# A PEER layer on one core: an early fetched tile in the routing stage, and a dense stage that steps all fetched tiles together with U in three fp32r passes

## What is computed

```
def blk(tb):                                   # 128 tokens
    q = (tb @ wq).reshape(128, 8, 2, 128)
    sc = einsum('thpd,pnd->thpn', q, subkeys)
    sv, si = top_k(sc, 16)
    cand = sv[:,:,0,:,None] + sv[:,:,1,None,:]
    cv, ci = top_k(cand.reshape(128, 8, 256), 16)
    e = i1 * 128 + i2                          # 128 experts a token, of 16384
    g = softmax(cv)
    h = einsum('thkd,td->thk', u[e], tb)
    a = gelu(h) * g
    return einsum('thk,thkd->td', a, v[e])
```

## Time and profile before

| | us |
|---|---|
| median of 3 runs | 3752.91 (3752.08 to 3759.64) |
| profiled execution | 3756.75 |
| its span, first to last instruction | 3755.0 |
| start of the dense stage in it | 1906 |
| start of the last PE instruction | 3745 |
| TensorE clock, mean granted share | 0.958 |

### The profile page before, as it was taken

The page is one execution under the profiler, slowest core; times in us unless marked ns, Lnnn a source line. Parts: engine busy times, 40 slices in busy tenths (PEclk is TensorE's granted clock), DMA queues, the critical chain, the costliest instruction groups (busy, mean ns, idle before and its releaser), DMA issues.

```text
span 3755.0 us, 45250 instructions
## 1 busy us (share of the span) xinstructions
PE 3435.2 (91%) x14374; PEld 2026.9 (54%) x14374; DVE 2662.5 (71%) x4988; ACT 890.0 (24%) x1844; POOL 1447.1 (39%) x1116
## 2 busy tenths in 40 slices
PE   8998989986889998999549999999999999999998
PEld 7444879884466667677414444444444444444443
DVE  0453887756368755655768888887888888889786
ACT  1452211215122338797100000100001000100001
POOL 0000187740232778874023343333343334333331
PEclk8899999988899999999779999999999999999999
DMA  7898499975887668888679999999999999999994
GB/s 262 342 421 298 136 401 378 378 275 168 322 311 252 170 179 182 193 147 190 205 285 398 406 398 390 398 390 391 409 385 400 406 397 418 401 399 365 387 379 185
DMA packets 470727, 1201.16 MB, mean 320 GB/s; under 512 B 196953, under 2 KB 261897, under 8 KB 391817
## 3 DMA queue, kind: packets, MB, share of 16 engines
q0 software_dynamic: 149776, 679.68, 47.7%
q1 hardware_dynamic: 187200, 498.50, 35.7%
q10 hardware_dynamic: 133568, 20.84, 3.5%
HBM read 1127.33 MB, written 72.61 MB: 320 GB/s over the span
## 4 chain that ended last, share of the span: by engine, by line
PE 32%; DVE 8%; issue 4%; DMA 4%; DVEq 1%; POOL 1%; POOLq 0%
PE d_ps L2482 17%; PE d_ps L2471 15%; DVE d_acc L2367 4%; DMA d_ring<-peer_uv,d_idx 3%; DVE d_ring L2353 3%; DMA out_y<-k_yacc 1%; DVE d_qacc L2384 1%; DVE k_yacc L2367 1%; POOL d_ring L2315 0%; DVE d_aw L2362 0%; DVE d_a L2375 0%; DVE d_qacc L2413 0%; DVEq L2362 0%; DVEq L2353 0%; DVEq L2366 0%
## 5 line engine op out<-in xcount | busy, mean ns | idle before, releaser
L2315 POOL DMA_INDIRECT d_ring<-peer_uv,d_idx x512 | 654.3, 1278 | 1067.1 <-DVEq L2369 964.1
L2471 PE MATMUL d_ps<-k_xd,k_ring 128*128 128x512 f32 x2048 | 907.0, 596 | 74.6 <-SPq L2283 60.4
L2471 PEld LDWEIGHTS d_ps<-k_xd,k_ring 128*128 128x128 f32 x2048 | 391.5, 191 | 569.4 <-issue 508.3
L2353 DVE SCALAR_TENSOR_TENSOR d_ring<-d_ring,k_xn 128x1024 f32<-128x1024 f32 x512 | 605.6, 1219 | 70.2 <-DMA d_ring<-peer_uv,d_idx 39.5
L2482 PE MATMUL d_ps<-d_v,d_a 128*128 128x512 f32 x1024 | 456.9, 600 | 32.5 <-DVE d_a L2375 24.6
L2482 PE MATMUL d_ps<-k_ring,d_a 128*128 128x512 f32 x1024 | 451.7, 594 | 16.1 <-DVE d_a L2375 16.1
L1630 POOL DMA_INDIRECT G<-c_cellg,c_cell x256 | 420.2, 1641 | 116.8 <-issue 90.1
L2367 DVE SCALAR_TENSOR_TENSOR d_acc<-d_ring,d_aw,d_acc 128x1024 f32<-128x1024 f32 x256 | 328.8, 1284 | 49.9 <-DVE d_acc L2367 32.3
L2367 DVE SCALAR_TENSOR_TENSOR k_yacc<-d_ring,d_aw,k_yacc 128x1024 f32<-128x1024 f32 x256 | 328.7, 1284 | 47.8 <-DVE k_yacc L2367 31.7
L2482 PEld LDWEIGHTS d_ps<-d_v,d_a 128*128 128x128 f32 x1024 | 196.3, 193 | 284.7 <-issue 283.4
L2438 ACT ACTIVATE d_ge<-d_h (+1 forms) x256 | 52.1, 203 | 1238.6 <-DVE d_ring L2353 1238.5
(11 more groups left out here) (382 smaller groups left out, 4442.3 us busy)
## 6 DMA issues: line engine op xcount, KB each, us to landing
c_chunk<-wq SPq DMA_DIRECT2D x128, 512.0 KB
k_ring<-u_blocks SPq DMA_DIRECT2D x128, 512.0 KB, 12.7
s_kc<-sb_kT SPq DMA_DIRECT2D x32, 1024.0 KB, 9.1
s_vc<-sb_v SPq DMA_DIRECT2D x32, 1024.0 KB, 7.3
c_chunk<-w_m SPq DMA_DIRECT2D x64, 512.0 KB
k_ring<-v_blocks SPq DMA_DIRECT2D x64, 512.0 KB, 13.4
d_gb<-G SPq DMA_DIRECT2D x32, 1024.0 KB
d_v<-v_blocks SPq DMA_DIRECT2D x64, 512.0 KB
```

Of the source, the lines that this page charges most:

```text
L2315: pool.indirect_dma_start(out=ring[:, b], out_offset=None, in_=a["peer_uv"], in_offset=bass.IndirectOffsetOnAxis(ap=idx8[par][:, b:b + 1], ...
L2353: last = nc.vector.scalar_tensor_tensor(ring[:, b, 0:D], ring[:, b, 0:D], 1.0, xn[T % 2][:], ALU.mult, ALU.mult, accum_out=h[:, bass.ds(co ...
L2471: last = nc.tensor.matmul(ps[:, HB + x % 2, :], ub[j][:, k], xd[:, k].rearrange("p t q -> p (t q)"), start=(k == 0), stop=(k == KC - 1))
```

## The change

In `decide`:

- The order of fates: tile 1 is now a fetched one; sent are tiles 2 and 4, hot 3 and 5, fetched 1, 6, 7, 8. `TILE` maps places in the intermediate buffers back to tiles.
- Tile 1's normed inputs stay in `c_xn0`. DVE's new `dots` multiplies its 128 fetched U rows (512 KB a slot) by them into `k_h0`: 16 in stage 4, 26, 31 and 33 in stages 5, 6 and 7, 22 in stage 8. The rows pass through three slots of the ring (`EB`). A row's gather waits until the dot three before it is done.
- POOL's queue: 19 of those gathers ahead of the first scatter, then one after each scatter with s % 5 in (0, 2, 4) of the first sent tile, and after s % 4 == 1 of the second: 19, 77 and 32. The two sent tiles' heads no longer take turns.
- One-hot chunks are moved between places, eight of them into the selection after the loop; six chunk buffers for weights become five; eight of the 56 V gathers for the sampled tile move forward into stage 2.

In `dense`:

- All fetched tiles step together: per PE block one 1 MB gather for each of tiles 6 to 8 and one 512 KB gather of V rows for tile 1, whose hidden values are already there. The ring of eight becomes two buffers per tile (`both`) and a single one for tile 1 (`values0`).
- `hidden` in three passes: ACT rounds a U block to fp32r (`u_high`), DVE subtracts (`low`, `u_low`), PE does 16 matmuls of `u_high` with both parts of the inputs and 8 of `u_low` with the high part.
- `values`: four of the eight outputs of a group stay in PSUM over the whole stage (`HELD`), so `take` runs four times a group.

```
+    BETWEEN, DOTS, DOTS_BESIDE = 29, {4: 16, 5: 20, 6: 19, 7: 21, 8: 10}, {5: 1, 6: 2, 7: 2, 8: 2}
-    NB = 6
+    NB = 5
     RB = 6
+    EB, EARLY_AT = 3, 3
...
+                def early_rows(n):
+
+                    for k in range(asked[0], min(asked[0] + n, P)):
+                        if k >= EB:
+                            pool.wait_ge(dotted, k - EB + 1)
+                        pool.indirect_dma_start(out=ring[:, EARLY_AT + k % EB], out_offset=None, in_=rows,
+                                                in_offset=bass.IndirectOffsetOnAxis(ap=row0[:, k:k + 1], axis=0)).then_inc(filled[EARLY_AT + k % EB], 16)
+                        asked[0] = k + 1
+
+                pool.wait_ge(rows_ready, 1)
+                pool.wait_ge(summed, REST)
+                early_rows(DOTS[4] + EB)
...
-                for h in range(4):
-                    scatter_head(0, h)
-                for h in range(4):
-                    scatter_head(1, h)
-                    scatter_head(0, h + 4)
-                for h in range(4):
-                    scatter_head(1, h + 4)
+                        if s % rows_after[0] in rows_after[1]:
+                            early_rows(1)
+
+                for h in range(8):
+                    scatter_head(0, h, (5, (0, 2, 4)))
+                for h in range(8):
+                    scatter_head(1, h, (4, (1,)))
+                early_rows(P)
...
+                def dots(n):
+
+                    for k in range(dots_done[0], dots_done[0] + n):
+                        s = EARLY_AT + k % EB
+                        dve.wait_ge(filled[s], 16 * (len(range(s, REST, RB)) + k // EB + 1))
+                        nc.vector.scalar_tensor_tensor(ring[:, s], ring[:, s], 1.0, xn0[:], ALU.mult, ALU.mult, accum_out=h0[:, k:k + 1]).then_inc(dotted, 1)
+                    dots_done[0] += n
...
+                        due = DOTS.get(i, 0)
+                        dots(due * passed[0] // BETWEEN - due * (passed[0] - 1) // BETWEEN)
...
                         one_hots(k)
+                        dots(DOTS_BESIDE.get(i, 0))
```

and in `dense`, on DVE, ACT and PE:

```
+                def low(b, j):
+
+                    dve.wait_ge(u_high_done, b + 1)
+                    if not (number(b) and b == 0):
+                        dve.wait_ge(h_done, b)
+                    nc.vector.tensor_tensor(u_low[:], ub[j], u_high[:].bitcast(F32), ALU.subtract).then_inc(u_low_done, 1)
...
+                            products(k, x)
                             gate(b - 1, y // GB, y % GB, k if x else k - 1)
...
+                            low(b, j)
+                        n = 2 * k + u - 1
+                        if j in (1, 2) and not (number(n) and n < 0):
+                            for c in (2 * j - 2, 2 * j - 1):
                                 take(n, c)
...
+                        add_rows(k, x)
...
                     for k in range(KC):
-                        last = nc.tensor.matmul(ps[:, HB + x % 2, :], ub[j][:, k], xd[:, k].rearrange("p t q -> p (t q)"), start=(k == 0), stop=(k == KC - 1))
+                        for n, x_part in enumerate((x_high, x_low)):
+                            last = nc.tensor.matmul(ps[:, HB + x % 2, :], u_high[:, k], x_part[:, k], start=(k == 0 and n == 0), stop=False)
+                    last.then_inc(high_used, 1)
+                    pe.wait_ge(u_low_done, b + 1)
+                    for k in range(KC):
+                        last = nc.tensor.matmul(ps[:, HB + x % 2, :], u_low[:, k], x_high[:, k], start=False, stop=(k == KC - 1))
```

## The result

The changed kernel takes 3887.22 us (median of 4 runs, 3884.22 to 3891.12); its ratio to the kernel before is 1.0356 (95% interval 1.0338 to 1.0374), so it is 3.6% slower. 3828 us was forecast, with a range of 3725 to 3965. The profiled execution has a span of 3889.4 us. The dense stage starts at 2199 us (forecast 2132, before 1906) and lasts 1690 us (forecast 1698, before 1849). So the dense stage gained 159 us as worked out, the routing stage lost 293 instead of 226, and the error of 59 us is 67 in the routing stage less 8 in the dense one.

The account below looks back on a forecast made before the run. PE was taken to bound the dense stage before, POOL's queue the changed routing stage. Dense start 2132 (226 later) plus 1698 dense (151 less) gives a 3830 span, 3828 us against the median, 2.0% slower; range 3725 to 3965.

Parts of the forecast that it names:

- PE's block of 12.31 us: Dense stage: PE's time per block falls from 13.73 to 12.31 us, as hidden takes 5.44 us instead of 6.87.
- The loop through the landings: Dense stage: issue, landing and gathers' data against shallow buffers add 0 to 1.4 us a block over 12.31; 0.5 taken.
- the low end: Dense block: period of 12.1 us with none of SP's 1.31 MB in the way, so no wait over 12.31.
- Head: Start of the dense stage until the first values: 75 us, before 73.
- fourth case: Rival, dense stage: loop bound by landings, 13.7 us a block instead of 12.8, 112 us more, 3940 us; chance 0.15.
- The takes: Dense block: DVE's takes wait for PE's block end, using most of 1.1 us of room; costed at nothing.
- POOL's sum: Routing stage: scatters, gathers and waits in POOL's queue take 743 us from 1254.4, ending at 1997; taken as the limit.
- 3 x 5 us at changes of stage: Routing stage: at three changes DVE's work between takes about 20 us against 15 for POOL's three rows and scatters.
- Alone this would add some 15 us: Routing stage: the 128 dots cost DVE 151 us; if POOL did not hold the stage, they would add some 15.
- up to some 10 us: Routing stage: five chunk buffers, moved V gathers and PE's clock costed at nothing; each up to this if POOL didn't hold it.
- POOL keeps up: Rival, routing stage: POOL's instructions cost less between gathers; delay about 50 us, 3652 us, or 3617 with only 15; chance 0.20.
- third case: Rival, routing stage: rough handover, POOL loses 25 us more at each of four changes of stage, 3928 us; chance 0.14.

Follow-up runs that it names:

- two passes: Changed kernel with the eight u_high times x_low matmuls per block left out, x_low still made: 3888.96 us, ratio 1.0357 to the kernel before.
- scatters alone: Changed kernel without the 128 early U-row gathers and without 127 of their 128 products on DVE: 3628.03 us, ratio 0.9672 to the kernel before.
- the two kernels without rows: Changed kernel without the 128 early U-row gathers, once with the products on DVE kept (3685.62 us), once with 127 of 128 left out too (3628.03 us).
- the kernel without the rows: Changed kernel without the 128 early U-row gathers, scatters kept, products still run on what lies in the slots: 3685.62 us, ratio 0.9787 to the kernel before.
- even rates: Changed kernel with three early rows after every seven scatters in both sent tiles and products of stages 6, 7, 8 at 17, 17, 16: 3862.68 us, ratio 1.0309.

## Why the prediction came out as it did

Slower was the likeliest case, with POOL's queue in the routing stage as the reason, and the runs show that reason: left alone with either half of its queue, POOL does not hold the stage. The size of the loss was too small: 75 us were forecast and 135 came. The forecast for the dense stage is close in part by luck: the period was 0.13 us longer than forecast, 16 us over the stage, and the head and the end were each some 12 us shorter. Step by step:

*Dense stage.* PE's block of 12.31 us: 12.32 where PE alone bounds. The loop through the landings, with ends of 12.1 and 13.7 us a block: 12.10 with the loads taken away, which is the low end's condition, and 12.93 with them, where 12.8 was taken. Head: 63 us to the first values (2199.2 to 2262.6) for 75. Stage: 1690 us for 1698. The subtraction is 1.22 us for 1.15. The prediction had this loop as a term on top of PE's block, and as its fourth case at full size. The runs show that the loop sets the period and PE's block does not (12.95 with two passes); the half microsecond that was taken over 12.31 was a choice between two ends that no row decided. The takes were costed at nothing; nothing in the waits speaks against it (1.7 us of idle time before them in 1300).

The Trainium skill ("DMA: Bandwidth & Descriptors", section on SWDGE vs HWDGE vs iDMA) says that GpSimd's queue and the hardware's share each DMA engine in turns. The prediction put the sum by it near 3940, but that is its 13.7 us a block, worked out with half of the loads in the way; all 1.31 MB at 417 GB/s would be 3.1 us, a block of 15.2. The loads lengthened the block by 0.83 us (12.10 to 12.93), about half of the 1.6 of the first and a quarter of the second, so an effect is there, but much smaller than loads fully in the way.

*Routing stage.* POOL's sum is the term that failed, by 73 us. It was 743 us from 1254.4, end at 1997; it was 796 us from 1274.5, end at 2070.4 (the last scatter starts at 2068.8). By parts:

| part of POOL's sum | forecast us | measured us |
|---|---|---|
| start of the scatters | 1254.4 | 1274.5 |
| scatters with the gap behind each, waits between heads | 573 | 446.4 + 73.7 + 43.5 = 563.6 |
| 109 gathers | 145 | 133.1 + 29.9 = 163.0 |
| waits for products | 25 | 69.2 |
| sum | 743 | 795.8 |

The scatters' cost hit by two errors that cancel: a scatter's mean was 1.74 us, not 1.62, so scatters and gaps were 520 us for 494, and the waits between heads were 43.5 us for the 79 in the sum, since gathers stand in them. A gather was 1.22 us (133.1/109), not 1.08. The first wait for a product was 23.9 us for 25. The step that was mis-sized most is the wait for products after it: 45 us in ten waits where none was in POOL's sum. It was reasoned about only on DVE's side, 3 x 5 us at changes of stage. 36 of the 45 us stand in one place, at and just behind the change from stage 6 to 7 (22.1, 4.9, 5.2 and 4.2 us). The start was 20 us late with tile 2's weights: 1259.6 without rows and products, 1266.8 with the products, 1274.5 with both. Stage 4 already holds 16 products, and the sum had taken the weights' time from before.

*Behind POOL.* The last residual came 11 us after POOL's last scatter (forecast 26), the dense stage 120 us after it (forecast 109; before 103). The 120 are not POOL's: they are 117.5 us in the kernel with scatters alone, so 14 of the 35 us that go to the new order and the buffers lie here.

*Products on DVE.* "Alone this would add some 15 us" was too low: 49 us by the two kernels without rows. The 35 us for all that was costed at nothing in this stage (order of tiles, chunk buffers) were within the "up to some 10 us" each only if there are three or four of them. Whether they show in the total while POOL holds the stage was not tried, but both belong in the case in which POOL keeps up: that rival's 3617 us would have been about 3686, which is what the kernel without the rows takes; it could hardly come out otherwise, as both corrections are from that kernel and the one with scatters alone.

**The signs.** POOL's last scatter near 2000: 2069. DVE idle for U rows, 60 to 100 us in each of stages 7 and 8: 87 and 98. PE under 75%: 61 and 65%. Of the third case's sign, POOL idle over 20 us at each change of stage, there were two, at the first (23.9, which the sum had) and from stage 6 to 7 (22.1); from 5 to 6 it was 7.2, from 7 to 8 none. That case would have added 100 us; 45 came. Of the fourth's, DVE waits for gathers in most blocks, the waits are there (142 in 128 blocks), but the DMA share is 0.98, not under 0.95. It reads 0.98 to 1.00 also where engines are not what limits, so it was no good sign. Here the prediction's fourth case was right in its mechanism and small in its size.

**The rival that POOL keeps up** rested on 1.4 us an instruction; 365 instructions took 796 us, 2.2 each, and 1.87 without any wait for a product or a landing. The Trainium skill (same page, "Latency and other measured facts") gives about 1 us of emission for a DMA from GpSimd. The scatter's median was 1.58 us, its mean 1.74: for scatters the trace does not agree. For the gathers of rows it does, with a median of 1.01 us.

None of these kernels that computes the whole layer beats the kernel before; the best, with even rates, is 3.1% slower.

## What to carry to other kernels

Slack of a queue engine is eaten at the price of its whole instruction, with the gap behind it and its mean rather than its median, and by the waits of an in-order partner: 109 gathers in a queue with 160 us of slack cost 163 us themselves and 69 us of waits, and DVE, which consumes them, stood for 285 us. Price such a move by leaving out each half of the queue in turn: here the rows cost some 30 to 45 us without the scatters and 210 us among them. In a loop whose buffers are one or two deep, work out the way from the last use through the issue and landing to the next use; it gave 12.1 us for the 12.10 measured without direct loads, and with them only two ends, 12.3 and 13.7, for 12.93. The share of busy transfer engines suggested a bound that removing bytes did not confirm.

## What the runs showed of the hardware

- A stretch with 0.98 of the DMA engines busy and 385 to 388 GB/s was not at their limit for this loop: with 0.26 MB of direct loads a block less it was 358 to 365 GB/s at a share of 0.92 to 0.94, and the block did not get shorter (13.09 us for 12.93).
- Three gathers of 8 KB rows and one of 4 KB rows a block, with nothing beside them, moved 305 GB/s at a share of 0.84, and the former took 8.4 us to land (median; 9.3 with 1.31 MB of direct loads a block beside them).
- TensorE's granted clock was 1.00 in the dense stage with PE busy for 97%, and 0.94 to 0.96 with the pass taken out and PE busy for 87 to 88% (2300 to 3300). PE's block of 10.5 us would be 81% of the period of 12.95, so part of what the shorter block frees went with the lower clock. In the routing stage it fell from 1.00 in stage 7 to 0.79, with PE busy for 61%.
- A scatter of 128 single floats is 1.55 us at the shortest in all kernels. Its mean is 1.64 us in the kernel before and with scatters alone, 1.79 with 128 products of 1.22 us on DVE beside them, and 1.74 with products and gathers of rows. A gather of 128 rows of 4 KB is 1.01 us in the median.
